# Four 64x64 tiles of TensorE for a chunked RWKV recurrence in both directions

## The reference

```python
def step(s, inp):                       # s is 64 x 64
    sa = einsum("bhvk,bhk->bhv", s, -kk_t)
    s = s * w_t + sa[..., None] * (kk_t * a_t) + v_t[..., None] * k_t
    return s, einsum("bhvk,bhk->bhv", s, r_t)
for d, rev in enumerate((False, True)):
    yc, s_ctx = scan(zeros, context tokens, reverse=rev)
    yl, _     = scan(s_ctx, latent tokens,  reverse=rev)
```

## Time and profile before

| | us |
|---|---|
| median of 3 runs | 2505.53 (2504.07 to 2506.45) |
| the profiled execution, its own time | 2504.86 |
| its span, first to last instruction | 2503.0 |
| PE busy | 2371.5 (95%) |
| DVE busy | 1595.3 (64%) |
| ACT busy | 1185.1 (47%) |
| POOL busy | 175.1 (7%) |
| granted TensorE clock, mean | 0.981 |

### The profile page before, as it was taken

How to read it: one execution, slowest core, us unless ns; L and a number is a source line. 1 busy time by engine, 2 the same in 40 slices (tenths; PEclk the granted TensorE clock), 3 DMA queues, 4 the chain that set the end, 5 groups by cost and what they waited for, 6 DMA issues and landing times.

```text
span 2503.0 us, 48578 instructions
## 1 busy us (share of the span) xinstructions
PE 2371.5 (95%) x20263; PEld 1845.7 (74%) x20263; DVE 1595.3 (64%) x1807; ACT 1185.1 (47%) x1268; POOL 175.1 (7%) x270
## 2 busy tenths in 40 slices
PE   5999889998999999999789989999999999999997
PEld 3446379964888787556689868888888888888886
DVE  3474556534333323484455459898989898989897
ACT  3331422212222223442322247777777777777774
POOL 0000044300000000000444000000000000000000
PEclk9999999999999999999999989999999999999998
DMA  7221700043233225222000559999999999999997
GB/s 284 67 84 68 269 3 4 21 186 101 84 101 101 84 85 201 95 82 68 2 4 21 220 181 375 331 371 339 369 341 367 340 366 344 367 341 366 340 368 261
DMA packets 234872, 500.77 MB, mean 200 GB/s; under 512 B 9446, under 2 KB 78332, under 8 KB 227676
## 3 DMA queue, kind: packets, MB, share of 16 engines
q1 hardware_dynamic: 232544, 484.24, 54.2%
q10 hardware_dynamic: 2172, 14.20, 1.5%
HBM read 492.12 MB, written 6.29 MB: 199 GB/s over the span
## 4 chain that ended last, share of the span: by engine, by line
PE 90%; DVE 3%; POOL 2%; issue 2%; ACT 1%; DMA 1%; ACTq 0%; POOLq 0%; DVEq 0%
PE ps L580 17%; PE ps L581 17%; PE ps L582 17%; PE ps L669 10%; PE ps L866 10%; PE ps L573 7%; POOL tail L2324 2%; PE ps L608 2%; PE ps L894 2%; PE ps L1145 1%; PE ps L1188 1%; PE ps L995 1%; PE ps L1154 1%; PE ps L1047 1%; DMA tail<-in_w_out 1%
## 5 line engine op out<-in xcount | busy, mean ns | idle before, releaser
L2219 DVE TENSOR_TENSOR weight_parts<-front,weight_parts 128x2048 fp32r<-128x2048 f32 x336 | 768.0, 2290 | 101.1 <-ACT weight_parts L1599 97.2
L1599 ACT ACTIVATE weight_parts<-front 128x2048 fp32r<-128x2048 f32 x336 | 643.6, 1920 | 252.5 <-PE ps L582 252.4
L580 PE MATMUL ps<-weight_parts,token_parts 128*128 128x512 f32 x1344 | 533.1, 397 | 1.9 <-issue 1.9
L581 PE MATMUL ps<-weight_parts,token_parts 128*128 128x512 f32 x1344 | 524.7, 390 | 0.0
L582 PE MATMUL ps<-weight_parts,token_parts 128*128 128x512 f32 x1344 | 524.6, 390 | 0.0
L1279 ACT ACTIVATE tail<-ps 128x512 f32<-128x512 f32 (+2 forms) x219 | 124.2, 569 | 393.6 <-DVE tail L1969 170.1
L580 PEld LDWEIGHTS ps<-weight_parts,token_parts 128*128 128x128 f32 x1344 | 253.0, 188 | 56.2 <-DVE weight_parts L2219 4.6
L582 PEld LDWEIGHTS ps<-weight_parts,token_parts 128*128 128x128 f32 x1344 | 252.8, 188 | 54.9
L581 PEld LDWEIGHTS ps<-weight_parts,token_parts 128*128 128x128 f32 x1344 | 253.2, 188 | 49.3
L866 PE MATMUL ps<-tail 64*64 64x64 f32 x7808 | 258.0, 220 | 32.4 <-POOL tail L2324 16.6
L669 PE MATMUL ps<-front,tail 128*128 128x512 f32 (+3 forms) x704 | 281.8, 556 | 6.5 <-ACT front L1354 4.4
(11 more groups left out here) (259 smaller groups left out, 2297.4 us busy)
## 6 DMA issues: line engine op xcount, KB each, us to landing
front<-in_exp_w SPq DMA_DIRECT2D x345, 1024.0 KB, 7.0
tail<-in_ffn_w SPq DMA_DIRECT2D x30, 1024.0 KB, 5.1
tail<-in_ada_w SPq DMA_DIRECT2D x27, 1024.0 KB, 8.6
tail<-in_w_in SPq DMA_DIRECT2D x24, 1024.0 KB, 5.1
front<-in_ada_w SPq DMA_DIRECT2D x21, 1024.0 KB, 12.1
tail<-in_w_out SPq DMA_DIRECT2D x8, 1024.0 KB, 6.5
parked_x<-front ACTq DMA_DIRECT2D x2, 2048.0 KB, 10.8
front<-parked_x ACTq DMA_DIRECT2D x2, 2048.0 KB, 8.7
```

Of the source, the lines that this page charges most:

```text
L580: mm(view, a_hi, b_hi, start=start, stop=False)
L581: mm(view, a_lo, b_hi, start=False, stop=False)
L1599: f_(whi[k % PARTS], at(A_RING2 + (k % RING2) * SLOT2, SLOT2), ACT.Copy).then_inc(cnt["act"].sem, 1)
L2219: ins = v.tensor_tensor(wlo[k % PARTS], at(A_RING2 + (k % RING2) * SLOT2, SLOT2), whi[k % PARTS], ALU.subtract)
```

## The change

Every product of `chunks` now uses all four 64x64 tiles. Direction 0 goes straight as before (operands in half `h`, result in half `h`). Direction 1 goes across: operands in half `h`, result in half `1-h`. The two directions of a product are written to two neighbouring banks (`to` and `to+1`), and the eight banks form four pairs: `P_T` for `level`, `P_X` for `doubled`, `P_SEQ` for `R`, `U`, `S`, `VT`, `BT`, `P_OUT` for `G`, `H`, `Y`, `KT`. The order inside a product becomes `cc`, `d`, `h`, so four matmuls in a row are on four tiles.

What follows from it: tiles of direction 1 are stored with halves exchanged where a product has crossed them once; ACT's copy of `XT` becomes three instructions, one for direction 0 and two of 64 partitions that exchange the halves of direction 1. Products of `S` with token arrays (`R'`, `Y'`, the parts with `cross=False`) stay straight in both directions, and the crossed part that adds to the same banks waits for them (`after_straight`). DVE's transpose becomes two halves, one for each direction, with a semaphore each. `begun` writes to a new tile `XI`, which ACT copies to `XT`; the first transpose is a step of its own (`first_turn`). `attention_norm` is split into reciprocals of 128 columns, two to a step. `R`'s product with `VT` moves from the end of a pass to the next pass, behind `doubled(1)`; `S`'s with `KT` moves behind `level(3)`; the last part of `Y` moves up.

```diff
-                def small(key, a, b, bank, begin=True, end=True):
-                    where = banks.take(pe, key, bank) if begin else psum[bank]
-                    for d in range(2):
-                        for cc in range(CC):
+                def small(key, a, b, to, begin=True, end=True, cross=True):
+                    if begin:
+                        banks.take(pe, key, to)
+                    for cc in range(CC):
+                        for d in range(2):
                             for h in range(2):
-                                ins = mm(piece(where, d, cc, r), a(d, cc, r), b(d, cc, r),
-                                         start=begin and d == 0 and cc == 0, stop=end, skip_group_check=True)
+                                r, r_out = halves[h], halves[(h + d) % 2 if cross else h]
+                                ins = mm(psum[to + d][r_out, cc * CH:(cc + 1) * CH], a(d, cc, r), b(d, cc, r),
+                                         start=begin and cc == 0, stop=end, skip_group_check=True)
                     if end:
                         banks.fill(ins, key)
+                    elif not cross:
+                        ins.then_inc(ev("straight"), 1)
...
                     if seq_ and n > 0:
                         banks.released(pe, ("S", l, n - 1))
-                        small(("R", l, n), tokens(Za, n), of(S), 2, begin=False)
-                    if pre:
-                        gram("G", n + 2, 0)
+                        small(("R", l, n), tokens(Za, n), of(S), P_SEQ, end=False, cross=False)
                     if inv:
                         doubled(1, n + 1)
+                    if seq_:
+                        banks.released(pe, ("VT", l, n))
+                        banks.released(pe, ("H", l, n))
+                        if n > 0:
+                            after_straight(n, 0)
+                        small(("R", l, n), half(AZAK[m], 0), of(VT[m]), P_SEQ, begin=n == 0)
                     if pre:
-                        gram("G", n + 2, 1)
+                        gram("G", n + 2)
...
+                def exchanged(dst, src):
+                    for h in range(2):
+                        ins = f_(dst[halves[h], 1].rearrange("p a b -> p (a b)"), src[halves[1 - h]], ACT.Copy)
+                    return ins
...
-                    act.wait_ge(ev("x_ready"), (LEVELS - 1) * (STEPS * l + n) + b + 1)
-                    out_of(("XT", l, n, b), XT[n % 2])
+                    bank = banks.see(act, ("XT", l, n, b))
+                    if b < LEVELS - 1:
+                        act.wait_ge(ev("x0_ready"), (LEVELS - 2) * (STEPS * l + n) + b)
+                    f_(XT[n % 2][:, 0].rearrange("p a b -> p (a b)"), pair(P_X)[:, 0], ACT.Copy)
+                    if b < LEVELS - 1:
+                        act.wait_ge(ev("x_ready"), (LEVELS - 1) * (STEPS * l + n) + b + 1)
+                    banks.done(exchanged(XT[n % 2], pair(P_X)[:, 1]), ("XT", l, n, b))
...
-                    v.transpose(every(X), bank).then_inc(ev("x_ready"), 1)
+                    v.transpose(flat(X, 0), pair(P_X)[:, 0]).then_inc(ev("x0_ready"), 1)
+                    v.transpose(flat(X, 1), pair(P_X)[:, 1]).then_inc(ev("x_ready"), 1)
```

More of the change, by code:

```diff
@@ L346, in hybrid_backbone, with pair @@
         MT = [both() for _ in range(N_MT)]
-        X, T1, RHS, UU, S, SW, DW = (both() for _ in range(7))
+        X, XI, T1, RHS, UU, S, SW, DW = (both() for _ in range(8))
+        P_T, P_X, P_SEQ, P_OUT = 0, 2, 4, 6
+        halves = slice(0, CH), slice(CH, P)
+        def pair(b, w=CC * CH):
+            return psum_all[:, b:b + 2, 0:w]
         zr, bk = at(A_Z, 4, CC * NTOK), at(A_Z + 8192, 4, CC * NTOK)
@@ L941, in chunks @@
                         banks.released(pe, ("XT", l, n, LEVELS - 1))
[L942 to L945, removed]
+                        small(("U", l, n), of(XT[m]), of(RHS), P_SEQ)
                     if inv:
@@ L1976, in begun, with first_turn @@
                                     ).then_inc(ev("xt_begun"), 1)
+                def first_turn(n):
                     dve.wait_ge(ev("xt_begun"), STEPS * l + n + 1)
-                    v.transpose(every(X), every(XT[n % 2])).then_inc(ev("x_ready"), 1)
+                    v.transpose(every(X), every(XI)).then_inc(ev("x_ready"), 1)
                 def state(n):
-                    bank = banks.see(dve, ("S", l, n))
+                    banks.see(dve, ("S", l, n))
+                    bank = pair(P_SEQ).rearrange("p a (b c) -> p a b c", b=CC)
@@ L2033, in chunks @@
                     if inv:
+                        level(4, n + 1)
+                    if pre:
+                        begun(n + 2)
+                    if inv:
+                        doubled(4, n + 1)
+                        gram("H", n + 1, 0)
                         level(5, n + 1)
-                    if n + 2 < STEPS:
-                        begun(n + 2)
-                    if 0 <= n < CC:
-                        attention_norm(n)
+                    if pre:
+                        first_turn(n + 2)
+                    if inv:
+                        gram("H", n + 1, 1)
             def finish(l):
@@ L2320, in level_mask @@
                             pool.wait_ge(ev("xt_begun"), STEPS * l_ + n_ + 1)
-                    for d in range(2):
-                        banks.released(pool, ("G", l, n, d))
+                    banks.released(pool, ("G", l, n))
                     for d in range(2):
@@ L2326, in level_mask @@
                     ins.then_inc(ev("mt_ready"), 1)
[L2328 removed]
+                banks.see(pool, ("G", l, 0))
                 for n in range(-2, STEPS):
```

171 lines of the change are left out of this document (94 added, 77 removed).

## The result

The changed kernel takes 2470.14 us (median of 4 runs, 2463.25 to 2473.43), the kernel before 2504.80 beside it. The ratio is 0.9858, 95% interval 0.9835 to 0.9881: faster by 1.4%, about 35 us. The forecast was 109 us. The profiled execution took 2468.93 us with a span of 2467.1.

A forecast was written before the change was run, and what follows sets the result against it. PE was taken to bound the stage. Seven steps saving 48.7 us in layer 0 and 49.0 in layer 1, plus shorter first inversions and last steps, made 108.8 us: 2504.9 to 2396 us, range 2360 to 2510.

The forecast's parts named there:

- What bounds the kernel now: The stage is PE's: busy 190.8 of layer 0's 199 us, a product 0.93, PE's sum 23.0 of a 23.95 us step.
- What a product on four tiles costs: Row and column halves both multiply at once, four records per 58 ns, so a product takes 0.46 instead of 0.93.
- Rivals 2 and 3: Four tiles run as two pairs, product 0.93, chance 0.16; weights of one column half wait, product 1.87, chance 0.12.
- rival 1: Dispatch holds PE at about 25 ns a record, product 0.80, step 19.9, time 2445; chance 0.20.
- The other new costs: Half transposes 0.44 each, ACT's three XT pieces 0.38 each, reciprocals of 128 columns 0.91; PE's sum 12.4, DVE's 14.5.
- A full step walked: Layer 0's step followed through levels and engines: 16.6 us, 17.0 on average; layer 1 15.9 to 16.3.
- the chain's 17.0: Average layer 0 step in us, set by the chain of levels with DVE in its place order.
- PE's sum after: 12.4 us: PE's work in a full step after the change: 19 products at 0.46, two at 0.93, two grams at 0.87.
- The sum: Seven steps save 48.7 us in layer 0 and 49.0 in layer 1; with first inversions and last steps 108.8, giving 2396.
- What would show it: Signs if right: product near 0.46, steps 16 to 17.5 us, PE at most 80% busy, its idle time ended by DVE.
- C: Rival raised after the measurement: the granted clock, 0.93, 0.76 and 0.91 in three of twelve steps, makes steps long; no chance given.

The follow-up runs named there:

- e5: Kernel of e2 plus one idle product behind each of the five XT products of a step, to keep PE busy: 2419.01 us, ratio 0.9659.
- e2: Changed kernel with all products but T and XT reading upper halves as bfloat16, one pass: 2426.52 us, ratio 0.9667.
- e4_streams: Separate kernel, computing nothing of the reference: streams of 64x64 products without waits, on two or four tiles; four tiles unrolled took 3.43 us for 256 instructions.
- e8_loops: Separate kernel, computing nothing of the reference: four-tile products with 128 columns unrolled, then loops of 1280 to 4096 instructions; 1280 took 2.19 us for 256.

## Why the prediction was wrong

**What bounds the kernel now.** "So this stage is PE's" was right, but PE's 0.93 a product had two causes that coincide: two tiles' time, 3.7 us for 256 instructions, and their supply, 3.4 to 3.7 us. The rows showed only the first.

**What a product on four tiles costs.** Right: 0.46. Rivals 2 and 3 fall with it, and so does rival 1 as a limit on starts: records run at 14.5 ns, four of them within 20 ns. The Trainium skill's floor of about 25 ns between starts ("TensorE: Matmul & The Clock Gate", Part 1) does not hold for these four tiles, where 32 records start in 0.46 us.

**The other new costs.** Right within 0.03 us: half transposes 0.449 and 0.407 (0.44 forecast), ACT's pieces 0.38 (0.38), reciprocals 0.927 (0.91).

**A full step walked.** This is the step that failed. The walk let PE run each product at 0.46 whenever its operands were there. It lacked a term: 1489 instructions of a step at 3.4 to 3.8 us per 256 are 20 to 22 us, over the chain's 17.0 and over PE's 12.4. Measured: 22.0; in layer 1, 5.3 blocks on average at 3.8 us are 20.0, measured 20.1. Where that floor is lifted and the clock holds, the walk comes out within half a microsecond: 16.5 to 17.4 us in five of six steps of e5 in layer 0 (the sixth took 18.9), 16.3 in one step of layer 1 of e2. Both have lighter products off the chain than the walk had, so this agreement is good but not exact. The sum "PE's sum after: 12.4 us" hid the term, since it counts an instruction only by what it does on the array.

**The sum.** Both stages together became 41.4 us shorter (19.0 and 22.4) instead of 108.8. The six counted steps gave 11.7 and 18.8 of that, where the walk had some 42 in each layer. The rest of the profiled execution was 5.5 us longer, which is as much as it differs from run to run. Rival 1's time, 2445, lay nearest, by luck: its mechanism was wrong.

**What would show it.** "All its idle time ended by DVE" was the sign that failed, and the one that told: 27.4 of 43.4 us were ended by "issue".

The Trainium skill tells of this supply ("Runtime: NRT & Kernel Launch", Instruction fetch mechanics): blocks of 16 KiB, 256 instructions, fetched through the sequencer's own DMA queue, at a cost that is mostly hidden. Blocks and queue are those of this case's trace. Hidden it was only at two tiles' pace; on four tiles e4_streams shows 10.8 us of 27.4 unhidden.

What stays open: the block price inside the changed kernel, 3.8 us on average in the twelve steps against 3.4 to 3.7 in the streams. The packets tell where it lies: in layer 0's steps PE goes on 2.4 us after a packet's start on average, as in the streams (2.4 to 2.6), but the next packet starts 1.44 us after that, 1.15 in the streams. PE's waits for DVE between two blocks would do that, and so would the three steps at a lower clock (C's part); no run separates the two.

## What to carry to other kernels

Beside each engine's busy time, count its instructions: unrolled code of small matmuls can't run faster than its program arrives, here 256 instructions per 3.4 to 3.8 us, and a float32 matmul on small tiles is four of them. An "issue" gap in the middle of a product that comes back every 256 instructions is the sign. Then a change pays by taking instructions out (one pass instead of two; one transpose of 128 rows, two instructions, instead of two products of 64 rows, eight), or by a loop whose body stays in the engine (seen here only in streams that compute nothing), and filling PE's waits with extra instructions is not free.

## What the runs showed of the hardware

PE's program is not fetched far ahead: 40 us of idle time bought no more than about one block, and no packet came in them (e4_streams). The same engine keeps much more behind it: a loop body of 1280 instructions ran from the second pass on without a fetch, one of 1664 in every other pass, one of 1920 never (e8_loops). Loads of some 400 GB/s stretched a block from 3.4 to about 6 us, with 3.8 and 4.1 us between two starts of PE in two of them. And in the faster kernels the granted clock came in: three steps of e2 had 0.50, 1.2 GHz, and took 19.4 to 20.2 us where a neighbour at 0.85 took 17.1, while the kernel before had 0.99 over the whole stage. What brings it down these runs don't show: the changed kernel's step at 339.1 us kept 1.00 with PE busy for 13.5 of its 20.0 us.
